# Where the products of the key norms stand among the tiles of the value projection in an RWKV layer

## What is computed

```
xr, xw, xk, xv, xa, xg = (h + xx * mu[j] for j in range(6))
r, k, v = xr @ w_rkv[0], xk @ w_rkv[1], xv @ w_rkv[2]
g = jax.nn.sigmoid(xg @ g1) @ g2
kk = heads(k * k_k)
kk = kk / jnp.maximum(jnp.linalg.norm(kk, axis=-1, keepdims=True), 1e-12)
for d in range(2):
    w = -jax.nn.softplus(-(w0[d] + jnp.tanh(xw @ w1[d]) @ w2[d])) - 0.5
    a = jax.nn.sigmoid(a0[d] + (xa @ a1[d]) @ a2[d])
    kd = k * (1.0 + (a - 1.0) * k_a)
```

## Time and profile before

| | us |
|---|---|
| median of 3 runs | 2829.89 (2829.07 to 2831.11) |
| profiled execution, its own time | 2832.73 |
| span of the profiled execution | 2830.9 |
| TensorE busy | 2588.6 (91%) |
| VectorE busy | 664.5 (23%) |
| ScalarE busy | 468.8 (17%) |

### The profile page before, as it was taken

How to read it: one execution, slowest core, us unless ns; L and a number is a source line. 1 busy time by engine, 2 the same in 40 slices (tenths; PEclk the granted TensorE clock), 3 DMA queues, 4 the chain that set the end, 5 groups by cost and what they waited for, 6 DMA issues and landing times.

```text
span 2830.9 us, 60504 instructions
## 1 busy us (share of the span) xinstructions
PE 2588.6 (91%) x27787; PEld 1795.2 (63%) x27788; DVE 664.5 (23%) x1098; ACT 468.8 (17%) x781; POOL 46.4 (2%) x146
## 2 busy tenths in 40 slices
PE   6998878999999778868888879999999999999997
PEld 2562732444444366857788569696969696969593
DVE  1033443000000266764776420000000010100001
ACT  3232012100000143443233120000000000000000
POOL 0000002200000000000000000000000000000000
PEclk9988989999999889989999789999999999999999
DMA  6215104522222320042001248888889898979793
GB/s 242 75 60 222 61 17 193 186 74 75 74 74 81 134 67 1 4 130 89 2 4 43 81 158 317 305 319 301 324 298 328 292 334 288 339 284 343 278 347 121
DMA packets 179204, 492.95 MB, mean 174 GB/s; under 512 B 9410, under 2 KB 73236, under 8 KB 172804
## 3 DMA queue, kind: packets, MB, share of 16 engines
q1 hardware_dynamic: 177156, 482.73, 47.8%
q0 software_dynamic: 1792, 6.19, 0.7%
HBM read 487.84 MB, written 1.05 MB: 173 GB/s over the span
## 4 chain that ended last, share of the span: by engine, by line
PE 86%; DVE 8%; ACT 3%; issue 2%; DMA 2%; SPq 0%; POOL 0%; DVEq 0%; ACTq 0%; POOLq 0%
PE banks L1022 24%; PE banks L1039 14%; PE banks L604 11%; PE banks L736 11%; PE banks L805 6%; PE banks L746 5%; PE banks L646 2%; PE banks L543 1%; PE banks L996 1%; PE banks L938 1%; DVE rstd L1363 1%; PE banks L1007 1%; PE banks L698 1%; PE banks L769 1%; PE banks L780 1%
## 5 line engine op out<-in xcount | busy, mean ns | idle before, releaser
L1022 PEld LDWEIGHTS banks<-ring_arena 128*64 128x64 f32 x14336 | 687.1, 137 | 19.1 <-issue 18.2
L1022 PE MATMUL banks<-ring_arena 128*64 128x112 f32 x14336 | 694.0, 259 | 0.0
L1039 PE MATMUL banks<-ring_arena 128*112 128x512 f32 x896 | 385.8, 592 | 0.0
L604 PE MATMUL banks<-ring_arena 128*128 128x256 f32 (+1 forms) x1024 | 314.5, 470 | 22.0 <-ACT ring_arena L1078 12.7
L736 PE MATMUL banks<-ring_arena 128*128 128x512 f32 x704 | 305.0, 596 | 0.0
L1039 PEld LDWEIGHTS banks<-ring_arena 128*112 128x112 f32 x896 | 158.0, 177 | 221.9 <-issue 221.9
L604 PEld LDWEIGHTS banks<-ring_arena 128*128 128x128 f32 x1024 | 199.6, 195 | 137.4 <-issue 96.2
L1868 DVE TENSOR_TENSOR ring_arena<-ring_arena,banks 128x448 f32<-128x448 f32 x32 | 19.9, 621 | 1033.1 <-PE banks L1022 1033.1
L736 PEld LDWEIGHTS banks<-ring_arena 128*128 128x128 f32 x704 | 134.7, 192 | 169.6 <-issue 169.6
L805 PE MATMUL banks<-ring_arena 64*64 64x128 f32 (+1 forms) x6144 | 203.3, 258 | 29.0 <-DVE ring_arena L1679 15.1
L805 PEld LDWEIGHTS banks<-ring_arena 64*64 64x64 f32 x6144 | 190.9, 137 | 36.2 <-issue 20.5
(11 more groups left out here) (293 smaller groups left out, 1847.4 us busy)
## 6 DMA issues: line engine op xcount, KB each, us to landing
ring_arena<-in_moe_w_gu SPq DMA_DIRECT2D x256, 896.0 KB, 5.5
ring_arena<-in_moe_w_d SPq DMA_DIRECT2D x112, 1024.0 KB, 7.1
ring_arena<-in_mod_w SPq DMA_DIRECT2D x48, 1024.0 KB, 7.4
ring_arena<-in_ff_w_gu SPq DMA_DIRECT2D x22, 1024.0 KB, 5.1
ring_arena<-in_rw_w_rkv SPq DMA_DIRECT2D x20, 1024.0 KB, 10.9
ring_arena<-in_gla_w_in SPq DMA_DIRECT2D x12, 1024.0 KB, 5.4
ring_arena<-in_ff_w_d SPq DMA_DIRECT2D x11, 1024.0 KB, 4.9
ring_arena<-in_gla_w_out SPq DMA_DIRECT2D x4, 1024.0 KB, 13.8
```

The lines of the kernel that those rows point to most:

```text
L604: ins = T.matmul(b[:, 0:width], w[:, k, j * P:j * P + P], src[:, k, :], start=(k == 0), stop=(k == KT - 1))
L1022: ins = T.matmul(bank[CH * h:CH * h + CH, (c % 4) * CAP:(c % 4) * CAP + CAP], w[:, kk, c * P + CH * h:c * P + CH * h + CH], XG[:, 2 * kp + ...
L1039: ins = T.matmul(ps[6 + h][0:CAP, :], HX[:, 2 * u + k, :], w[:, k, 512 * h:512 * h + 512], start=(u == 0 and k == 0), stop=(u == WD_UNITS ...
```

## The change

`project` takes a function that is called ahead of each tile, and the 8 products of the key norms are handed to the value projection in that way. The products, their waits and their banks are the same as before. Product 0 stands ahead of value tile 0, products 1 and 2 ahead of tile 1, 3 and 4 ahead of tile 2, 5 and 6 ahead of tile 3, and 7 ahead of tile 4. The blocks of the other engines are not changed.

```diff
-            def project(cid, src, width, n_chunks):
+            def project(cid, src, width, n_chunks, between=None):
 
                 for i in range(n_chunks):
                     arrived(pe, cid + i)
                     w = slot(cid + i, KT)
                     for j in range(2):
+                        if between:
+                            between(2 * i + j)
                         b = next_bank()
...
                 project(first[f"rw_k{sg}"], mix(sg), SEG, 4)
-                for p in range(HP):
-                    pe.wait_ge(S["k_sq"], HP * sg + p + 1)
-                    if p >= 2 or sg:
-                        pe.wait_ge(S["kn_max"], HP * sg + p - 1)
-                    T.matmul(ps[6 + p % 2][:, 0:SEG], HEAD_ONES[:, :], sq[:, (p % 2) * TOK:(p % 2) * TOK + SEG],
-                             start=True, stop=True).then_inc(S["kn_mm"], 1)
-                project(first[f"rw_v{sg}"], mix(sg), SEG, 4)
+
+                def key_norms(n):
+                    for p in ((0,), (1, 2), (3, 4), (5, 6), (7,), (), (), ())[n]:
+                        pe.wait_ge(S["k_sq"], HP * sg + p + 1)
+                        if p >= 2 or sg:
+                            pe.wait_ge(S["kn_max"], HP * sg + p - 1)
+                        T.matmul(ps[6 + p % 2][:, 0:SEG], HEAD_ONES[:, :], sq[:, (p % 2) * TOK:(p % 2) * TOK + SEG],
+                                 start=True, stop=True).then_inc(S["kn_mm"], 1)
+                project(first[f"rw_v{sg}"], mix(sg), SEG, 4, key_norms)
```

## The result

| | before | changed |
|---|---|---|
| median of 4 runs, us | 2829.55 (2829.07 to 2831.11) | 2807.49 (2807.25 to 2809.99) |
| span of the profiled execution | 2830.9 | 2805.9 |

The ratio is 0.992, with a 95% interval of 0.9905 to 0.9934: 22.1 us faster, where 18.2 us were forecast (2811.7, range 2806.5 to 2817.5). The sign and the place were right, and the gain is 3.9 us larger than the sum.

The account below looks back on a forecast made before the run. TensorE was taken as the bound, held at VectorE's pace through the key norms. Gains of 6.95 us in segment 0 and 11.2 us in segment 1 sum to 18.15 us, giving a median of 2811.7 us, range 2806.5 to 2817.5.

Parts of the forecast that it names:

- What bounds the stretch: Key norms between key and value projection: TensorE waits at VectorE's pace, 14.52 us; pauses of 0.95 and 0.5 us would stay.
- Segment 0, VectorE sets the end: Segment 0 up to its scan: VectorE, 2.67 us later, sets the opening; first scan matmuls come 8.55 us earlier.
- Cold start: Start of segment 0's scan: TensorE idles 5 us before it, so one group of `raw` runs at half clock, costing 1.61 us.
- Segment 1: Value to gate projections of segment 1: TensorE stays the bound and warm, VectorE's work hidden by 6 us; gain 11.2 us.
- Sum: Whole kernel: 6.95 us from segment 0 plus 11.2 us from segment 1, 18.15 us less, median 2811.7.
- the second rival: Segment 0 to its scan: VectorE isn't later and the scan starts warm; 23 us gained, 2807; chance 0.12.
- The offset from span to median: Whole kernel: the profiled execution lay 2.84 us over the timed median 2829.89, so 2814.5 own time became a median of 2811.7.
- The first: Pauses in the value stretches: clock lost, one fall in each segment gives 2816, two give 2820.5; chance 0.15.
- The third: Keys' chain in both segments: it follows TensorE's tiles step by step, so no gain in the end, 2829.9; chance 0.04.
- The fourth: Value stretches: half clock stays throughout, 19.5 us more in each segment, 2869; chance 0.03.

Follow-up runs that it names:

- the pairs: Against the changed kernel, products 0 and 1, 2 and 3, 4 and 5, 6 and 7 stand ahead of value tiles 0 to 3; ratio to before 0.9931.
- the changed kernel kept warm: The changed kernel with ten more products, results unused, behind the value projection of segment 0; ratio to before 0.992.
- the warm pairs: Two products ahead of each of value tiles 0 to 3, three semaphore instructions fewer, six unused products behind segment 0's value projection; ratio to before 0.9927.

## Why the prediction was right, and what it missed

- **What bounds the stretch.** Right. VectorE's pace held TensorE for 14.5 us; with tiles between the products only 0.90 and 0.47 us of pauses stay, against 0.95 and 0.5 worked out.
- **Segment 0, VectorE sets the end.** Right, and shown by the pairs. The delay of reciprocal 0 was 2.83 us (2.67 forecast), the gain to scan 0 8.28 us (8.55).
- **Cold start.** Right in kind: the first scan matmuls ran at half clock. Its cost was 1.3 us, 1.6 forecast: scan 0 as a whole is 1.33 us longer, and the third group of its matmuls already starts 8.65 us after the first (1108.44 - 1099.79), where it was 7.35 us before (1118.15 - 1110.80). When TensorE was kept busy 1.3 + 2.6 us of scan 0 went, and the 2.6 us lie outside this step.
- **Segment 1.** 10.78 us, 11.2 forecast, TensorE the bound to the end, VectorE 6.32 us ahead (6 forecast).
- **Sum.** 8.28 - 1.33 + 10.78 = 17.7 us against 18.15. The term that was missing is the end of the program. The prediction took it that nothing behind the scans depends on the change but its start. In fact the moved products need four semaphore instructions fewer; without these a jump of TensorE's behind the last matmul takes 0.23 us instead of 7.1, and the last 9.3 us became 3.9: 5.4 us, a quarter of the measured 22.1. 17.7 + 5.4 - 0.8 (rest) = 22.3, though "rest" varies by more than the 0.8 us, so that the close match is partly luck. So is it that 2807.5 us lies inside the range, 1 us above its lower end: that end was put there for the second rival and not for a shorter end of the program.
- **The offset from span to median.** The 2.84 us by which the profiled execution lay over the median were taken as an offset. Layer 0 alone puts product 0 anywhere from 1058.77 to 1066.89 in these profiles, so an offset of 2.84 us from one execution is no more than chance. It did no harm, since the forecast amounts to the median less the sum.
- **Rivals.** The first did not happen: the clock stood at 1.00 through both value stretches. The rule of the Trainium skill (TensorE: Matmul & The Clock Gate, "A second HAM failure mode: psum-queue depth-cycling") doesn't hold here at pauses of 0.5 to 0.9 us. The second gave a time, 2807, that was met by luck; its mechanism, TensorE alone counting, is ruled out by 38.02 us to scan 0. The third came true only where the products were placed late. The fourth was never seen.

## What to carry to other kernels

Put the small products of a chain that runs over several engines between the large tiles of the next independent work, and place them by what the other engines have queued: here one product too late made VectorE 2.8 us late, and products placed later still took nearly all of the gain away. When TensorE no longer sets the end of a stretch, look at what idles next and at its clock there. And compare the last microseconds of two programs, and their counts of instructions, before a gain of a few us is put down to the order of the work.

## What the runs showed of the hardware that I had not expected

- The end of the program went with the number of instructions: with 60499 and 60500 it took 3.84 to 3.93 us from the last row of residual additions on, with 60502 and 60504 7.89 to 9.29, and the difference is one jump over a skipped body of 6.1 to 7.6 us instead of 0.23. It isn't simply the longer the worse: the changed kernel kept warm, with 60540 instructions and 234 loads of them, had 3.88 us, and the warm pairs, with 60523 and 236, had 8.45.
- In scan 0, the time follows the mean clock: 122.5 us at 0.99, 125.1 at 0.96, 126.4 at 0.94. Three falls of the clock further in, which the kernel before has too, were absent when TensorE was kept busy ahead of the scan.
